# Who splits the down weights of an expert: VectorE's third split goes to GpSimd, and ScalarE's copy of the turned activation goes to VectorE

## The reference

```python
# _moe_swiglu, in words of the reference: top 2 of 8 experts per token
logits = h @ router + router_b           # 256 x 8
p      = softmax over the two largest    # weight of each chosen expert
for e in range(8):                       # EXPERT_DIM = 1408
    y_e = (silu(h @ w_gate[e]) * (h @ w_up[e])) @ w_down[e]
out = sum over the chosen e of p[e] * y_e
```

## Time and profile before

| what | value |
|---|---|
| time, median of 3 runs | 2355.15 us (2354.71 to 2356.49) |
| profiled execution | 2355.15 us, its span 2353.4 us |
| TensorE busy (matmul) | 2106.5 us, 90% |
| VectorE busy | 1496.8 us, 64% |
| ScalarE busy | 1080.9 us, 46% |
| GpSimd busy | 452.6 us, 19% |
| expert steps | from 1890.5 to about 2340 us |

### The profile page before, as it was taken

How to read it: one execution, slowest core, us unless ns; L and a number is a source line. 1 busy time by engine, 2 the same in 40 slices (tenths; PEclk the granted TensorE clock), 3 DMA queues, 4 the chain that set the end, 5 groups by cost and what they waited for, 6 DMA issues and landing times.

```text
span 2353.4 us, 36888 instructions
## 1 busy us (share of the span) xinstructions
PE 2106.5 (90%) x14422; PEld 1984.6 (84%) x14422; DVE 1496.8 (64%) x1958; ACT 1080.9 (46%) x1567; POOL 452.6 (19%) x187
## 2 busy tenths in 40 slices
PE   6999987999999995899895887999986799999997
PEld 6998977899899894899794887899885798898886
DVE  4555876555555656555657435555576578888887
ACT  4334533444433434433443113444445367677775
POOL 2222212222222220222220222222230000000000
PEclk9999989999999997999997887999998789999999
DMA  8554411455455450455541002455450368888885
GB/s 309 188 187 154 151 54 55 164 189 191 152 189 188 159 188 0 153 188 188 177 149 39 1 1 91 158 190 188 153 208 8 124 243 304 311 305 298 308 306 197
DMA packets 73264, 400.57 MB, mean 170 GB/s; under 512 B 8240, under 2 KB 8368, under 8 KB 41136
## 3 DMA queue, kind: packets, MB, share of 16 engines
q1 hardware_dynamic: 72704, 397.22, 49.3%
q10 hardware_dynamic: 432, 1.57, 0.2%
HBM read 397.71 MB, written 1.05 MB: 169 GB/s over the span
## 4 chain that ended last, share of the span: by engine, by line
PE 83%; DVE 11%; ACT 3%; issue 2%; POOL 0%; DMA 0%; DVEq 0%; SPq 0%; PEld 0%; ACTq 0%; PEldq 0%
PE psum L283 24%; PE psum L284 23%; PE psum L285 23%; DVE w_lo L267 2%; PE psum L686 2%; PE psum L694 1%; PE psum L2115 1%; PE psum L699 1%; PE psum L327 1%; DVE hT_lo L348 1%; ACT O L297 1%; PE psum L2128 1%; DVE O L929 1%; DVE O L343 1%; ACT w_hi L260 0%
## 5 line engine op out<-in xcount | busy, mean ns | idle before, releaser
L267 DVE TENSOR_TENSOR w_lo<-ring,w_hi 128x1024 fp32r<-128x1024 f32 x496 | 764.2, 1567 | 390.7 <-ACT w_hi L260 390.1
L260 ACT ACTIVATE w_hi<-ring 128x1024 fp32r<-128x1024 f32 x744 | 743.5, 1050 | 396.3 <-PE psum L285 252.8
L273 POOL TENSOR_TENSOR w_lo<-ring,w_hi 128x1024 fp32r<-128x1024 f32 x160 | 404.5, 2528 | 1194.9 <-ACT w_hi L260 1194.9
L283 PE MATMUL psum<-hT_hi,w_hi 128*128 128x256 f32 x2096 | 592.0, 282 | 23.8 <-DVE hT_lo L348 17.1
L284 PE MATMUL psum<-hT_lo,w_hi 128*128 128x256 f32 x2096 | 590.7, 282 | 0.0
L285 PE MATMUL psum<-hT_hi,w_lo 128*128 128x256 f32 x2096 | 590.3, 282 | 0.0
L283 PEld LDWEIGHTS psum<-hT_hi,w_hi 128*128 128x128 f32 x2096 | 399.9, 191 | 30.5 <-issue 23.7
L283 PE MATMUL psum<-w_hi,hT_hi 128*128 128x256 f32 (+1 forms) x1216 | 388.2, 319 | 38.2 <-issue 22.3
L284 PEld LDWEIGHTS psum<-hT_lo,w_hi 128*128 128x128 f32 x2096 | 399.9, 191 | 3.9
L285 PEld LDWEIGHTS psum<-hT_hi,w_lo 128*128 128x128 f32 x2096 | 400.0, 191 | 0.0
L285 PE MATMUL psum<-w_hi,hT_lo 128*128 128x256 f32 (+1 forms) x1216 | 375.9, 309 | 0.0
(11 more groups left out here) (442 smaller groups left out, 2051.3 us busy)
## 6 DMA issues: line engine op xcount, KB each, us to landing
ring<-in_stream SPq DMA_DIRECT2D x248, 1024.0 KB, 5.3
ring<-in_stream SPq DMA_DIRECT2D x248, 512.0 KB, 4.3
tables<-in_tables SPq DMA_DIRECT2D x1, 2517.0 KB, 20.1
gain_row<-in_gains ACTq DMA_DIRECT2D x3, 512.0 KB, 3.7
rows<-in_rows SPq DMA_DIRECT2D x1, 1288.0 KB, 23.0
X<-in_x SPq DMA_DIRECT2D x1, 1024.0 KB, 4.9
result<-X SPq DMA_DIRECT2D x2, 512.0 KB, 2.7
columns<-in_columns SPq DMA_DIRECT2D x1, 993.0 KB, 14.6
```

What stands on the lines that cost most here:

```text
L260: act.activation(part(w_hi, g, i), ring[:, k, i * PART:(i + 1) * PART], ACT.Copy) \
L267: dve.tensor_tensor(part(w_lo, g, i), ring[:, k, i * PART:(i + 1) * PART], part(w_hi, g, i).bitcast(F32), ALU.subtract) \
L273: pool.tensor_tensor(part(w_lo, g, 2), ring[:, k, 2 * PART:STEP], part(w_hi, g, 2).bitcast(F32), ALU.subtract) \
L283: pe.matmul(out_, w[0], x[0], start=first, stop=False, skip_group_check=True)
```

## The change

1. lo of part 2 (split_lo_last) leaves VectorE's iteration; a new function moe_pool gives it to GpSimd for all 88 steps, in order, outside the branch by load. The first wait of VectorE's expert part goes.
2. act_hi, the rounded copy of the turned activation, goes from ScalarE to VectorE (tensor_copy out of PSUM), right ahead of act_lo, and with it the waits for the turn and for the place in act_hi.
3. ScalarE does both early parts of g+2 in one row ahead of the jobs.
4. VectorE does lo of part 0 of g+2 ahead of all jobs, the results too.

```diff
@@ moe_scalar / experts_scalar
                 if g + 2 < total:
-                    split_hi(act, g + 2, g + 2, (0,))
-                for x, what, p in jobs(m, tiles):
-                    if what == "result":
-                        result(x, x % 2, g - 1)
-                if g + 2 < total:
-                    split_hi(act, g + 2, g + 2, (1,))
+                    split_hi(act, g + 2, g + 2, (0, 1))
                 for x, what, p in jobs(m, tiles):
                     if what == "piece" and p % 2 == 0:
                         piece(x, x % 2, p)
-                act.wait_ge(turned_ready, m + 1)
-                act.wait_ge(steps_used, g - 1)
-                act.activation(act_hi[:, f % 2, 0:slots], psum[:, UP_BANK + f % 2, 0:slots], ACT.Copy).then_inc(ffn_gated, 1)
+                    elif what == "result":
+                        result(x, x % 2, g - 1)
                 if g + 1 < total:
                     split_hi(act, g + 1, g + 1, (2,))
...
+        def moe_pool(pool, at):
+            for g in range(moe_first, total):
+                split_lo_last(pool, g, g)
@@ experts_vector
-            dve.wait_ge(lo_last_ready, moe_first)
...
-                split_lo_last(dve, g, g)
-                for x, what, p in jobs(m, tiles):
-                    if what == "result":
-                        result(x, x % 2)
                 if g + 2 < total:
                     split_lo(dve, g + 2, g + 2, (0,))
                 for x, what, p in jobs(m, tiles):
-                    if what == "pick":
+                    if what == "piece" and p % 2:
+                        piece(x, x % 2, p)
+                    elif what == "pick":
                         pick(x)
+                    elif what == "result":
+                        result(x, x % 2)
                     elif what == "chunk":
                         chunk(x, p)
-                    elif what == "piece" and p % 2:
-                        piece(x, x % 2, p)
+                dve.wait_ge(turned_ready, m + 1)
+                dve.wait_ge(steps_used, g - 1)
+                operand = psum[:, UP_BANK + f % 2, 0:slots]
+                dve.tensor_copy(act_hi[:, f % 2, 0:slots], operand).then_inc(ffn_gated, 1)
                 dve.wait_ge(ffn_gated, 2 * f + 2)
-                dve.tensor_tensor(act_lo[:, f % 2, 0:slots], psum[:, UP_BANK + f % 2, 0:slots], act_hi[:, f % 2, 0:slots].bitcast(F32), ALU.subtract) \
+                dve.tensor_tensor(act_lo[:, f % 2, 0:slots], operand, act_hi[:, f % 2, 0:slots].bitcast(F32), ALU.subtract) \
                    .then_inc(ffn_act_ready, 1)
@@ block.gpsimd
+                elif kind == "moe":
+                    moe_pool(pool, at)
```

## The result

The changed kernel takes 2423.6 us (median of 4 runs, 2418.2 to 2425.4) against 2354.9 for the kernel before in the same session: the ratio is 1.029, 95% interval 1.0276 to 1.0303, 69 us slower. The forecast was 2395 with a range up to 2420. It had the sign and the exclusion of the splits right and is 29 us short: its sum has no term for TensorE's clock, which fell.

A forecast was written before the change was run, and what follows sets the result against it. TensorE was taken to bound the expert stage, busy 422.8 of 440 us. Losses 31 + 4.4 + 6.6 + 2.2 = 44, less 4 for races, gave +40 on 2355: 2395 us, range 2366 to 2420.

The forecast's parts named there:

- the exclusion of the splits: Expert stage: splits of VectorE and GpSimd exclude each other, whichever starts first; one step needs 4.6 us of exclusive work, before 3.4.
- The forecast row of the table: Predicted step lengths of one middle expert, turn to turn, 4.34 to 7.5 us, together 61.7 us against 56.6 before.
- The two-step loop: Bare and chunk steps: VectorE's second split waits for GpSimd's, so two steps take at least 10.0 us, 5.0 a step.
- The start: Ahead of the loop: GpSimd's first split falls among VectorE's four of 4.62 us and holds up the logits by 2.2.
- Step 1: Second step of an expert: GpSimd's request is older, VectorE's split waits, down product 2.1 us late; 3.0 lost by step 3's turn.
- The walk: The prediction's count of waits and times through an expert's steps from a turn, losing 5.1 us a middle expert.
- only splits exclude each other: Claim that copy, gated, act_lo, y_lo, chunks and pieces run free beside GpSimd's split.
- The clock: Rival: TensorE's clock falls at stalls of 2.2 us, adding 14 to 29 us, 2405 to 2425; chance 0.12.
- The walk's own 44: Summed loss in us: six experts 31, the first 4.4, the last 6.6, ahead of the loop 2.2.
- The 4 us taken off for races: Step 0's request goes to GpSimd by 0.3 us only; VectorE assumed to get it in two of seven experts.
- the shorter latencies: Cast 0.5 us earlier, first step's act_lo 0.2, the 0.2 behind it gone: 6 us less if splits do not exclude, 2349.
- The second rival: Only the 5.0 us loop, VectorE winning at steps 0 and 1: 26 us slower, 2381, or 2370; chance 0.16.
- The loads: Loads costed at nothing: early load 2 us later in the step, needed three steps on; late load 7.4 after a turn.

The follow-up runs named there:

- Experiment 1: Changed kernel with each of GpSimd's 88 expert-layer instructions treating 8 columns and not 1024, all waits and other instructions kept: 2351.4 us, ratio 0.998.
- experiment 3: Changed kernel with lo of the last third back on VectorE behind gated, GpSimd idle, copy and orders as changed: 2357.6 us, ratio 1.0007.
- experiment 9: Changed kernel with the pick of the next expert in step 4 and not in step 1: 2395.8 us, ratio 1.0167.
- experiment 4: Changed kernel with 8 filler matmuls ahead of an expert's first up product and of step 1's down product, to hold the clock: 2402.0 us, 1.0204.
- experiment 10: Changed kernel with the pick in step 4 and 8 filler matmuls ahead of an expert's first up product alone: 2391.4 us, ratio 1.0149.
- experiment 2: Kernel before with only lo of the last third moved to GpSimd, act_hi on ScalarE and all orders kept: 2395.0 us, ratio 1.0169.

## Why the prediction was right and wrong

**The exclusion of the splits: right, shown.** Experiment 1 takes GpSimd's work away and the loss is gone; experiment 3 gives it back to VectorE, keeps all else and loses nothing. The forecast row of the table is met within 0.3 us a step by the kernel with the clock held, 61.9 against 61.7 an expert.

**The two-step loop: right.** Chunk steps come in pairs of about 4.8 and 5.2, 5.0 on average, and the last expert's bare steps too (4.80 and 5.17 in the trace).

**The start: right.** Ahead of the loop the four VectorE splits take 6.80 where the earlier trace rows has 4.62, GpSimd's one among them, 2.2 more:

```profile
1869.04 6.80 DVE L267 TENSOR_TENSOR w_lo<-ring,w_hi 128x1024 fp32r<-128x1024 f32 x4
1869.72 2.77 POOL L273 TENSOR_TENSOR w_lo<-ring,w_hi 128x1024 fp32r<-128x1024 f32 x1 [25.23 <-ACT w_hi L260]
```

**Step 1: right in length, wrong in cause.** The walk gave the second meeting to GpSimd and held VectorE's split back for 2.3 us. It was VectorE's by 0.05 to 0.15 us in every middle expert. And the sentence "only splits exclude each other" was false: the pick's copy, which has SBUF on both sides, was shut out for 2.35 us instead. The two errors cancel by luck: the pair of splits, one behind the other, ends at about the same time in either order, and m_now waited for that end. With VectorE first and no pick behind it act_lo is on time, as experiment 9 and the last expert show. In the last expert the errors do not cancel: the walk gave the last expert 6.6 us of loss, and it lost 5.0 (49.7 against 44.7).
The rule of the Trainium skill that the prediction drew on ("SBUF — State Buffer", "SBUF: two separate sides") names a second kind of VectorE instruction that takes the shared ports, those in a 2-port mode. By that rule m_now and m_pick would be shut out if they ran in such a mode; the traces agree (2.35 and 2.41 us), though they do not show the mode. The prediction used half of the rule.

**The clock: the step that failed.** It stood among the rivals with a chance of 0.12 and 14 to 29 us, against it the stalls of 1.38 us that had no fall behind them. So the sum put the fall at nothing. It was no rival but the other half of the same stalls, which the walk itself put at 2.2 and 2.1 us: the clock fell 13 times in the stage, and experiment 4 gives 22.7 us for it. The rival's own price of up to 1.8 us a fall was a little high, as matmuls of the up product followed each other by 0.21 us at 0.50 and by 0.12 at 1.00, not by twice as much. The walk's own 44 with the 22.7 makes 67, the measured loss is 69. The 4 us taken off for races that might go to VectorE were nothing to take off: VectorE won them and the loss stayed. That the 44 is so near the 46.0 of experiment 4 is in part luck, with the last expert 1.6 too high and the first 2.0 too low (4.4 against 60.0 less 53.6 in experiment 4).

**Where the 69 us are:** 22.7 the clock (experiment 4), 10.8 the pick behind GpSimd's split in step 1 (4 against 10: 46.0 less 35.2), 35.2 the rest: the splits in turn and, by the estimate at experiment 10, some 5 us of pick. The traces, from first turn to last, give 20.6, 9.9 and 32.9, with 2.2 ahead of them. The rest also holds whatever the shorter latencies give back; experiment 1 shows a gain of 4.6, but with VectorE relieved of a split as well, so their part alone is not shown.

**A rival's sum.** The second rival's 2381 follows from its terms. Its 2370, with small pieces at 5.0, does not: without the 0.9 for them it comes to 2375.

**The loads: right.** ScalarE waited for no transfer in the changed kernel, with 265 GB/s where it was 300. What I had not seen is that early_used, for which ScalarE's early splits wait, stands behind the down product in TensorE's program (line 2185). Each late act_lo made the next hi late as well, where these waits came to 1.8 us before:

```profile
ACT w_hi L260 <- PEq L2185: 17.4, 14, 3.0
```

So the stall of step 1 gives VectorE no lead. What that alone costs is not shown.

## What to carry to other kernels

Moving an elementwise instruction from VectorE to GpSimd takes it off VectorE's queue only where VectorE then works on PSUM operands; where both read and write SBUF their times add up, and GpSimd's 2.4 us stood for 1.2. Look for the short instructions too: one copy of 128 x 4 elements in the queue waited as long as a split. When a walk through the waits gives TensorE new stalls, price the clock with them: here two stalls of 2 us an expert cost half as much again (22.7 us beside 46.0).

## What was not expected of the hardware

- A VectorE copy of 128 x 4 elements between SBUF places took 2.31 to 2.36 us beside GpSimd's split and 0.16 without; a 128 x 128 compare 2.41 and 0.28. Copies out of PSUM were not touched: 0.68 for the cast at 2086.63, with GpSimd's split running from 2086.47.
- In the changed kernel TensorE fell to 0.50 of its clock at 13 of 14 stalls of 1.9 to 3.1 us; at the seven of 1.36 to 1.38 in the kernel before it never did. Behind the stalls of 1.93 the fall came 0.7 to 0.9 us after TensorE was at work again. The length of a stall does not settle it: in experiment 9 five of seven stalls of 1.9 us had a fall, in experiment 2 three of seven of 2.14, in experiment 10 neither of two of 2.1. What does is open.
- Which engine came first in step 1 was decided by 0.05 to 0.15 us, the same way in every middle expert.
